# The first loads in two queues, chunk 0 rounded first, and the squares of x behind the third block: a two-block transformer on one core

## The chip, the cores and the metric

The kernel runs on one core of one Trainium2 chip. The metric is the device time in microseconds, the median over timed runs. PE is the matmul engine, DVE the vector engine, ACT the scalar engine, POOL GpSimd; SP is the engine that issues most DMAs.

## What is computed

Two transformer blocks in float32 over 256 tokens of width 1024. Only the very start matters here: the norm of x and the projection with `w_in`.

```python
def rms_norm(x, g):
    xf = x.astype(jnp.float32)
    y = xf * lax.rsqrt(jnp.mean(xf * xf, axis=-1, keepdims=True) + EPS)
    return (y * g.astype(jnp.float32)).astype(x.dtype)

def token_mix(h, w_in, ...):
    p = (h @ w_in).astype(jnp.float32)
    (fox_qkv, fox_f, gdn_qkv, gdn_b, gdn_a, gdn_z, hg_q, hg_f, hg_i, hg_g,
     gla_qk, gla_v, gla_gk, gla_g) = jnp.split(p, _cut_points(IN_SIZES), axis=-1)
...
x = x + token_mix(rms_norm(x, norm1_g[l]), w_in[l], ...) @ w_out[l]
x = x + conv_glu_ffn(rms_norm(x, norm2_g[l]), ...)
```

## The kernel before

Every matmul operand is split in two: a high part, rounded on ACT to the matmul's format (`w_hi`, `h_hi`), and a low part, the remainder, made on DVE (`w_lo`, `h_lo`). A product is then three matmuls: high by high, low weights by high, high weights by low. Weights stream as blocks of 1 MB (128 partitions x 2048 elements, 8 chunks of 256 columns) through a ring of three slots: a DMA into `raw`, ACT's rounding (`split` on ACT, counted by `hi_ready`), DVE's remainder (`split` on DVE, counted by `lo_ready`), and PE's use (counted by `block_used`). SP loads block n when the low part of block n - 3 is done (`weights_in`).

The order of work on every engine is the order in which the code is written; engines meet only at semaphores. x lies in SBUF as 8 chunks of 128 channels by 256 tokens. The norm is not applied to x before the projection: x times the gain of its channel is multiplied, and the result is scaled per token by the reciprocal root `r_1`, which needs the sum of the squares of x over all chunks.

At the start, SP issues the gains (`channel[:, 0:KC]`), then x and the first real block (block 1, slot 1) in four quarters each, alternating, with the small weights (block 0, 28 columns, slot 0) in between, then block 2 in two halves. `first_chunks` on ACT rounds, for each quarter, the weights and two chunks of x, and squares the two chunks. DVE makes the remainders, and sums the squares (`sum_of_three`, `sum_of_last`, `fold_sum`) in between. On PE, `keep_busy` multiplies zeros 13 times, `first_columns` multiplies block 1 chunk by chunk with the small products woven in, `mean_of_x` sums the squares over the partitions by a matmul with ones, and `project(n, f)` multiplies one half (24 matmuls) of block n. ACT's `rstd_x` turns the mean into `r_1` by a logarithm and an exponential. DVE then scales the small products (`small_t`), which PE transposes (`turn_small`, L872) and multiplies (`gk_product`). PE's order from there is project(2, 1), project(3, 0), project(3, 1), gates, and so on; DVE goes on with scaling and convolution taps (L2385) of the projected blocks, which also wait for ACT's first tap and for the masks.

Of the kernel before, what the change touches and what calls it, by code (L numbers as in the profile page):

```python
# [16 lines left out]
P = 128  # L17
# [104 lines left out]
def build(nc, weights, small_in, x_in, masks_in, ident_in, channel_in, row_in, w_gk_in, p_in, table_in,  # L122
# [4 lines left out]
    with ExitStack() as ctx:  # L127
# [318 lines left out]
        def _(sp):  # L446
            sp.dma_start(channel[:, 0:KC], channel_in[:, 0:KC]).then_inc(sem("gains_loaded"), 16)
            for b in range(4):
                sp.dma_start(x[:, 2 * b:2 * b + 2, :], x_in[:, 2 * b:2 * b + 2, :]).then_inc(sem(f"x_loaded{b}"), 16)
                quarter = slice(b * BLK // 4, (b + 1) * BLK // 4)  # L450
                sp.dma_start(raw[:, 1, quarter], weights[0][:, quarter]) \
                    .then_inc(sem(f"x_loaded{b}") if b < 3 else raw_loaded[1], 16)
                if b == 0:
                    sp.dma_start(raw[:, 0, 0:KC * SMALL], small_in).then_inc(raw_loaded[0], 16)
            for half, done in enumerate((sem("half_loaded"), raw_loaded[2])):
                part = slice(half * BLK // 2, (half + 1) * BLK // 2)
                sp.dma_start(raw[:, 2, part], weights[1][:, part]).then_inc(done, 16)
# [78 lines left out]
        def _(pe):  # L536
# [296 lines left out]
            def first_columns():  # L833


                def small_products(k):
# [7 lines left out]
                    if k == KC - 1:  # L844
                        last.then_inc(block_used, 1)

                for k in range(KC):
                    if k % 2 == 0 and k < 6:
                        pe.wait_ge(sem("quarter_lo"), k // 2 + 1)
                    for lo in range(2):  # L850
                        pe.wait_ge(lo_chunk if lo else hi_chunk, k + 1)
                        if k == 6 and lo == 0:
                            block_ready(1)
                        a = h_lo if lo else h_hi
                        for f in range(2):
                            at = slice(k * 256 + f * P, k * 256 + (f + 1) * P)
                            o = PS[:, 5, f * TOK:(f + 1) * TOK]
                            last = add(o, w_hi[:, 1, at], a[:, k, :], k == 0 and f == 0 and lo == 0, k == KC - 1 and lo == 1)
                            if lo == 0:
                                add(o, w_lo[:, 1, at], a[:, k, :])  # L860
                    if k >= 2 and k < KC - 1:
                        small_products(k - 2)
# [2582 lines left out]
```

## Time and profile before

| what | value |
|---|---|
| median of 3 timed runs | 1015.18 us (1014.27 to 1016.13) |
| span of the profiled execution | 1012.9 us |
| median less span (issue and end around the span) | 2.3 us |
| PE busy | 999.3 us, 99% of the span |
| DVE, ACT busy | 846.0 us (84%), 618.7 us (61%) |
| HBM traffic | 174 GB/s over the span |

The profiled execution has no timed figure of its own; its span stands beside the median of the timed ones. In a timeline row the first figure is the start in us, the second the time from the start of the first to the end of the last instruction of the row; "idle before <-releaser" is how long the engine stood before it and what ended that. Neighbouring instructions of an engine overlap a little, so the distance of two starts is the better price of one.

### The profile page before, as it was taken

The page shows a single profiled execution, that of the slowest core. Times are in us where ns is not written, and L with a number is a line of the kernel's source. Part 1 is how long each engine was busy: PE and PEld are TensorE (multiplying, and loading weights), DVE is VectorE, ACT ScalarE, POOL GpSimd, SP SyncE. Part 2 cuts the span into 40 slices and gives each one's busy share as a digit, 9 for nine tenths or more (in the row PEclk, how much of TensorE's full clock was granted, in tenths as well). Part 3 has the DMA queues.
Part 4 walks back from the last instruction along what each step waited for, and adds up shares of the span by engine and source line. Part 5 has one row for each costly group of instructions (what it writes and reads, how often), then busy time and mean ns, then how long its engine had stood idle before and what let it go on. Part 6 is the DMA issues. An engine that isn't in the chain of part 4 may idle for free.

```text
span 1012.9 us, 20813 instructions
## 1 busy us (share of the span) xinstructions
PE 999.3 (99%) x8343; PEld 935.8 (92%) x8343; DVE 846.0 (84%) x1217; ACT 618.7 (61%) x852; POOL 5.8 (1%) x16
## 2 busy tenths in 40 slices
PE   8999999999999999999999999999999999999996
PEld 7998999999999998899999999999999999999985
DVE  6974896899988878869999888799776899988876
ACT  6753565657565655457565556675676666555565
POOL 0000000000000000000000000000000000000000
PEclk9999999999999999999999999999999999999998
DMA  8533315455555545657656555345445356655531
GB/s 328 185 117 96 126 48 176 166 206 172 209 202 171 202 149 184 208 209 231 213 172 209 203 173 201 125 167 184 150 132 174 129 173 210 209 201 186 187 125 42
DMA packets 26498, 175.99 MB, mean 174 GB/s; under 512 B 3229, under 2 KB 3509, under 8 KB 6080
## 3 DMA queue, kind: packets, MB, share of 16 engines
q1 hardware_dynamic: 25616, 171.31, 48.6%
q0 software_dynamic: 816, 3.73, 1.3%
q8 instruction: 50, 0.82, 0.3%
q14 instruction: 16, 0.13, 0.0%
HBM read 173.97 MB, written 2.63 MB: 174 GB/s over the span
## 4 chain that ended last, share of the span: by engine, by line
PE 84%; DVE 7%; ACT 3%; issue 2%; DMA 2%; SPq 0%; DVEq 0%; ACTq 0%
PE PS L587 71%; PE PS L538 12%; DVE w_lo L2244 2%; ACT w_hi L1503 2%; DMA arena<-masks_in 1%; DMA raw<-weights 1%; DVE arena L3051 1%; DVE arena L3024 1%; DVE arena L2385 1%; PE PS L1408 0%; DVE arena L3062 0%; DVE arena L2795 0%; DVE arena L3061 0%; DVE arena L3045 0%; DVE arena L3041 0%
## 5 line engine op out<-in xcount | busy, mean ns | idle before, releaser
L587 PE MATMUL PS<-h_store,w_hi 128*128 128x256 f32 (+1 forms) x1840 | 478.2, 338 | 1.3 <-DVE w_lo L2299 0.9
L2244 DVE TENSOR_TENSOR w_lo<-raw,w_hi 128x2048 fp32r<-128x2048 f32 x154 | 352.5, 2290 | 52.4 <-ACT w_hi L1503 47.2
L587 PE MATMUL PS<-h_store,w_lo 128*128 128x256 f32 (+1 forms) x1400 | 369.5, 281 | 0.2
L1503 ACT ACTIVATE w_hi<-raw 128x2048 fp32r<-128x2048 f32 x156 | 297.9, 1910 | 79.1 <-PE PS L587 64.4
L587 PEld LDWEIGHTS PS<-h_store,w_hi 128*128 128x128 f32 x1840 | 305.3, 187 | 41.0 <-DVE w_lo L2299 1.3
L587 PEld LDWEIGHTS PS<-h_store,w_lo 128*128 128x128 f32 (+1 forms) x1400 | 254.8, 188 | 0.8 <-DVE h_store L2858 0.6
L587 PE MATMUL PS<-act_hi,w_hi 128*128 128x256 f32 x704 | 195.7, 280 | 0.1
L587 PE MATMUL PS<-act_hi,w_lo 128*128 128x256 f32 x704 | 195.1, 279 | 0.1
L587 PE MATMUL PS<-act_lo,w_hi 128*128 128x256 f32 x704 | 192.0, 279 | 0.0
L587 PEld LDWEIGHTS PS<-act_hi,w_hi 128*128 128x128 f32 x704 | 132.3, 188 | 1.6 <-DVE act_hi L2858 0.6
L587 PEld LDWEIGHTS PS<-act_hi,w_lo 128*128 128x128 f32 x704 | 132.3, 188 | 0.3 <-DVE act_hi L2858 0.3
L587 PEld LDWEIGHTS PS<-act_lo,w_hi 128*128 128x128 f32 x704 | 130.5, 188 | 0.0
L1926 ACT ACTIVATE arena<-PS 128x512 f32<-128x512 f32 x51 | 30.2, 592 | 86.8 <-PE PS L587 86.8
L587 PE MATMUL PS<-w_hi,h_store 128*128 128x256 f32 (+1 forms) x352 | 71.4, 307 | 0.4 <-issue 0.4
L1918 ACT ACTIVATE arena<-arena,channel 128x256 f32<-128x256 f32 x132 | 63.6, 531 | 13.3 <-DVE arena L2952 12.0
L2929 DVE SCALAR_TENSOR_TENSOR arena<-arena,channel 128x254 f32<-128x254 f32 x132 | 58.0, 481 | 7.6 <-DVE arena L2925 0.3
L2925 DVE SCALAR_TENSOR_TENSOR arena<-arena,channel 128x255 f32<-128x255 f32 x132 | 57.7, 479 | 0.4 <-ACT arena L1918 0.4
L587 PEld LDWEIGHTS PS<-w_hi,h_store 128*128 128x128 f32 x352 | 54.4, 188 | 3.4 <-issue 0.4
L2950 DVE TENSOR_TENSOR arena<-PS,arena 128x512 f32<-128x512 f32 x51 | 35.0, 686 | 20.5 <-ACT arena L1926 20.5
L587 PE MATMUL PS<-w_lo,h_store 128*128 128x256 f32 (+1 forms) x176 | 45.7, 302 | 0.4 <-DVE w_lo L2244 0.4
L538 PE MATMUL PS<-h_store,w_hi 128*128 128x256 f32 x256 | 45.4, 279 | 0.0
L538 PE MATMUL PS<-arena 64*64 64x64 f32 (+8 forms) x1356 | 41.5, 224 | 0.0
(361 smaller groups left out, 1106.6 us busy)
## 6 DMA issues: line engine op xcount, KB each, us to landing
raw<-weights SPq DMA_DIRECT2D x155, 1024.0 KB, 4.9
raw<-weights SPq DMA_DIRECT2D x12, 256.0 KB, 3.9
arena<-masks_in SPq DMA_DIRECT2D x1, 1600.0 KB, 12.1
bias_by_key<-bias_by_distance POOLq DMA_DIRECT2D x1, 1536.0 KB, 8.0
x<-x_in SPq DMA_DIRECT2D x4, 256.0 KB, 4.4
raw<-weights SPq DMA_DIRECT2D x2, 512.0 KB, 9.0
arena<-bias_by_key POOLq DMA_DIRECT2D x1, 1024.0 KB, 6.7
result<-arena SPq DMA_DIRECT2D x4, 256.0 KB, 2.1
```

The costliest lines, as they stand in the source:

```text
L538: return pe.matmul(o, lhs, rhs, start=start, stop=stop)
L587: return pe.matmul(o, lhs, rhs, start=start, stop=stop, skip_group_check=True)
L1503: act.activation(w_hi[:, slot, :], raw[:, slot, :], ACT.Copy).then_inc(hi_ready, 1)
L1918: ins = act.activation(dst[:, c, :], src[:, c, :], ACT.Identity, scale=w, bias=b)
L1926: act.activation(low, PS[:, bank:bank + 2, TOK:512], ACT.Copy).then_inc(sem("low_copied"), 1)
L2244: tt(w_lo[:, slot, :], raw[:, slot, :], w_hi[:, slot, :].bitcast(F), ALU.subtract).then_inc(lo_ready, 1)
L2385: mark(stt(dst, PS[:, bank_of_block(n), f * TOK:(f + 1) * TOK - d], ch("gdn_conv", (3 - d) * 6 + 2 * s + f), dst, ALU.mult, ALU.add))
L2925: stt(y[:, c, 1:TOK], src[:, c, 0:TOK - 1], channel[:, bass.ds(col(1) + c, 1)], y[:, c, 1:TOK], ALU.mult, ALU.add).then_inc(ready[0], 1)
L2929: ins = stt(y[:, c, 2:TOK], src[:, c, 0:TOK - 2], channel[:, bass.ds(col(0) + c, 1)], y[:, c, 2:TOK], ALU.mult, ALU.add)
L2950: tt(z, PS[:, bank:bank + 2, 0:TOK], low, ALU.add).then_inc(sem("parts_added"), 1)
L3024: tt(z, PS[:, bank:bank + 2, 0:TOK], low, ALU.add).then_inc(sem("parts_added"), 1)
L3051: mark(stt(y_gate[:, c, back:TOK], y_up[:, c, 0:TOK - back], ch("sc_conv", (2 - back) * 8 + 2 * i + c), y_gate[:, c, back:TOK], ALU.mult, ...
```

## The change

x is now loaded from ACT's own queue, in a first quarter, a second quarter and a half, with the gains between the second quarter and the half. SP's queue carries the first block in two quarters and a half, and block 2 whole. ACT rounds chunk 0 of x before the first weights, and alternates on; the squares of x and their sums move behind the rounding and the remainders of block 2, the rounding of block 3 (`block_hi(3)`) moves ahead of `rstd_x`, and DVE's remainder of block 3 ahead of the scaling of the small products. On PE the order inside a chunk changes, the small products come in two groups of four, and `project(2, 0)` stands ahead of `mean_of_x`.

```diff
@@ -444,17 +444,14 @@
 
         @block.sync
         def _(sp):
-            sp.dma_start(channel[:, 0:KC], channel_in[:, 0:KC]).then_inc(sem("gains_loaded"), 16)
-            for b in range(4):
-                sp.dma_start(x[:, 2 * b:2 * b + 2, :], x_in[:, 2 * b:2 * b + 2, :]).then_inc(sem(f"x_loaded{b}"), 16)
-                quarter = slice(b * BLK // 4, (b + 1) * BLK // 4)
-                sp.dma_start(raw[:, 1, quarter], weights[0][:, quarter]) \
-                    .then_inc(sem(f"x_loaded{b}") if b < 3 else raw_loaded[1], 16)
-                if b == 0:
-                    sp.dma_start(raw[:, 0, 0:KC * SMALL], small_in).then_inc(raw_loaded[0], 16)
-            for half, done in enumerate((sem("half_loaded"), raw_loaded[2])):
-                part = slice(half * BLK // 2, (half + 1) * BLK // 2)
-                sp.dma_start(raw[:, 2, part], weights[1][:, part]).then_inc(done, 16)
+            def first_block(a, b, loaded):
+                sp.dma_start(raw[:, 1, a * 256:b * 256], weights[0][:, a * 256:b * 256]).then_inc(loaded, 16)
+
+            first_block(0, 2, sem("w_loaded0"))
+            first_block(2, 4, sem("w_loaded1"))
+            sp.dma_start(raw[:, 0, 0:KC * SMALL], small_in).then_inc(raw_loaded[0], 16)
+            first_block(4, KC, raw_loaded[1])
+            sp.dma_start(raw[:, 2, :], weights[1]).then_inc(raw_loaded[2], 16)
             sp.dma_start(ident[:, :], ident_in).then_inc(sem("ident_and_channel"), 16)
             sp.dma_start(channel[:, KC:N_PC], channel_in[:, KC:N_PC]).then_inc(sem("ident_and_channel"), 16)
             def weights_in(n):
@@ -842,28 +839,32 @@
                     add(o, w_lo[:, 0, at], h_hi[:, k, :])
                     last = add(o, w_hi[:, 0, at], h_lo[:, k, :], False, k == KC - 1)
                     if k == KC - 1:
-                        last.then_inc(block_used, 1)
+                        last.then_inc(block_used, 2)
 
                 for k in range(KC):
-                    if k % 2 == 0 and k < 6:
+                    at = [slice(k * 256 + f * P, k * 256 + (f + 1) * P) for f in range(2)]
+                    o = [PS[:, 5, f * TOK:(f + 1) * TOK] for f in range(2)]
+                    pe.wait_ge(hi_chunk, k + 1)
+                    if k in (0, 2):
+                        pe.wait_ge(sem("quarter_hi"), k // 2 + 1)
+                    if k == 4:
+                        pe.wait_ge(hi_ready, 2)
+                    for f in range(2):
+                        add(o[f], w_hi[:, 1, at[f]], h_hi[:, k, :], k == 0 and f == 0)
+                    if k in (0, 2):
                         pe.wait_ge(sem("quarter_lo"), k // 2 + 1)
-                    for lo in range(2):
-                        pe.wait_ge(lo_chunk if lo else hi_chunk, k + 1)
-                        if k == 6 and lo == 0:
-                            block_ready(1)
-                        a = h_lo if lo else h_hi
-                        for f in range(2):
-                            at = slice(k * 256 + f * P, k * 256 + (f + 1) * P)
-                            o = PS[:, 5, f * TOK:(f + 1) * TOK]
-                            last = add(o, w_hi[:, 1, at], a[:, k, :], k == 0 and f == 0 and lo == 0, k == KC - 1 and lo == 1)
-                            if lo == 0:
-                                add(o, w_lo[:, 1, at], a[:, k, :])
-                    if k >= 2 and k < KC - 1:
-                        small_products(k - 2)
-                small_products(KC - 3)
-                small_products(KC - 2)
-                small_products(KC - 1)
-                last.then_inc(block_used, 1)
+                    if k == 4:
+                        pe.wait_ge(lo_ready, 2)
+                    for f in range(2):
+                        add(o[f], w_lo[:, 1, at[f]], h_hi[:, k, :])
+                    pe.wait_ge(lo_chunk, k + 1)
+                    for f in range(2):
+                        add(o[f], w_hi[:, 1, at[f]], h_lo[:, k, :], False, k == KC - 1)
+                    if k == 3:
+                        for j in range(4):
+                            small_products(j)
+                for j in range(4, KC):
+                    small_products(j)
 
             def turn_small():
                 pe.wait_ge(sem("ident_and_channel"), 48)
@@ -1217,8 +1218,8 @@
             pe.wait_ge(*once("zeros"))
             keep_busy(13, 4)
             first_columns()
+            project(2, 0)
             mean_of_x(0, 6, sum_1, True)
-            project(2, 0)
             turn_small()
             gk_product()
             project(2, 1)
@@ -1555,23 +1556,31 @@
             def first_chunks():
 
 
+                def high(c):
+                    act.activation(h_hi[:, c, :], x[:, c, :], ACT.Identity, scale=ch(PREP[0], c)).then_inc(hi_chunk, 1)
+
+                def weights_hi(a, b, done):
+                    act.activation(w_hi[:, 1, a * 256:b * 256], raw[:, 1, a * 256:b * 256], ACT.Copy).then_inc(done, 1)
+
+                for b in range(2):
+                    act.wait_ge(sem(f"x_loaded{b}"), 16)
+                    high(2 * b)
+                    act.wait_ge(sem(f"w_loaded{b}"), 16)
+                    weights_hi(2 * b, 2 * b + 2, sem("quarter_hi"))
+                    high(2 * b + 1)
+                act.wait_ge(raw_loaded[0], 16)
+                act.activation(w_hi[:, 0, 0:KC * SMALL], raw[:, 0, 0:KC * SMALL], ACT.Copy).then_inc(hi_ready, 1)
+                act.wait_ge(sem("x_loaded2"), 16)
+                high(4)
+                act.wait_ge(raw_loaded[1], 16)
+                weights_hi(4, KC, hi_ready)
+                for c in range(5, KC):
+                    high(c)
+                act.wait_ge(raw_loaded[2], 16)
+                act.activation(w_hi[:, 2, 0:BLK // 2], raw[:, 2, 0:BLK // 2], ACT.Copy).then_inc(sem("quarter_hi"), 1)
+                act.activation(w_hi[:, 2, BLK // 2:BLK], raw[:, 2, BLK // 2:BLK], ACT.Copy).then_inc(hi_ready, 1)
                 for b in range(4):
-                    act.wait_ge(sem(f"x_loaded{b}"), 32 if b < 3 else 16)
-                    if b == 3:
-                        act.wait_ge(raw_loaded[1], 16)
-                    quarter = slice(b * BLK // 4, (b + 1) * BLK // 4)
-                    act.activation(w_hi[:, 1, quarter], raw[:, 1, quarter], ACT.Copy) \
-                        .then_inc(sem("quarter_hi") if b < 3 else hi_ready, 1)
-                    for c in (2 * b, 2 * b + 1):
-                        act.activation(h_hi[:, c, :], x[:, c, :], ACT.Identity, scale=ch(PREP[0], c)).then_inc(hi_chunk, 1)
-                    if b == 1:
-                        act.wait_ge(raw_loaded[0], 16)
-                        act.activation(w_hi[:, 0, 0:KC * SMALL], raw[:, 0, 0:KC * SMALL], ACT.Copy).then_inc(hi_ready, 1)
                     act.activation(sq4[:, b, :], flat(x[:, 2 * b:2 * b + 2, :]), ACT.Square).then_inc(sem("x_squares"), 1)
-                act.wait_ge(sem("half_loaded"), 16)
-                act.activation(w_hi[:, 2, 0:BLK // 2], raw[:, 2, 0:BLK // 2], ACT.Copy).then_inc(sem("quarter_hi"), 1)
-                act.wait_ge(raw_loaded[2], 16)
-                act.activation(w_hi[:, 2, BLK // 2:BLK], raw[:, 2, BLK // 2:BLK], ACT.Copy).then_inc(hi_ready, 1)
 
             def rstd_x(p, bank, dst, squared=None):
 
@@ -1624,14 +1633,19 @@
                     act.activation(flat(act_hi[:, 2 * b:2 * b + 2, :]), PS[:, 4 + b, :], ACT.Copy).then_inc(sem("mixed_hi"), 1)
 
             flat = lambda v: v.rearrange("p u n -> p (u n)")
+            for at, n in ((0, 2), (2, 2)):
+                act.dma_start(x[:, at:at + n, :], x_in[:, at:at + n, :]).then_inc(sem(f"x_loaded{at // 2}"), 16)
+            act.dma_start(channel[:, 0:KC], channel_in[:, 0:KC]).then_inc(sem("gains_loaded"), 16)
+            act.dma_start(x[:, 4:KC, :], x_in[:, 4:KC, :]).then_inc(sem("x_loaded2"), 16)
             act.preload_act_table_set(TABLES)
             act.wait_ge(sem("gains_loaded"), 16)
             act.wait_ge(*once("eps_set"))
-            first_chunks()
-            rstd_x(0, 6, (r_1, r_1_col))
-
             def block_hi(n):
                 split(n, n % RING, n // RING + 1)
+
+            first_chunks()
+            block_hi(3)
+            rstd_x(0, 6, (r_1, r_1_col))
 
             def tokens_from(n):
 
@@ -1824,7 +1838,6 @@
                 act.activation(a_la[CHUNK:P, :, CHUNK:P], a_packed[CHUNK:P, :, :], ACT.Copy) \
                     .then_inc(sem("diagonals_spread"), 1)
 
-            block_hi(3)
             gdn_last_tap(0, 1)
             gates()
             gk_logs()
@@ -2290,29 +2303,31 @@
                     tt(act_lo[:, 2 * b:2 * b + 2, :], pair(4 + b), act_hi[:, 2 * b:2 * b + 2, :].bitcast(F), ALU.subtract) \
                         .then_inc(sem("mixed_split"), 1)
 
-            for b in range(4):
-                quarter = slice(b * BLK // 4, (b + 1) * BLK // 4)
-                if b < 3:
-                    dve.wait_ge(sem("quarter_hi"), b + 1)
-                else:
-                    dve.wait_ge(hi_ready, 2)
-                tt(w_lo[:, 1, quarter], raw[:, 1, quarter], w_hi[:, 1, quarter].bitcast(F), ALU.subtract) \
-                    .then_inc(sem("quarter_lo") if b < 3 else lo_ready, 1)
+            def first_lo(a, b, done):
+                tt(w_lo[:, 1, a * 256:b * 256], raw[:, 1, a * 256:b * 256], w_hi[:, 1, a * 256:b * 256].bitcast(F), ALU.subtract) \
+                    .then_inc(done, 1)
+
+            for b in range(2):
+                dve.wait_ge(sem("quarter_hi"), b + 1)
+                first_lo(2 * b, 2 * b + 2, sem("quarter_lo"))
                 chunk_lo(0, 2 * b)
                 chunk_lo(0, 2 * b + 1)
-                if b == 1:
-                    dve.wait_ge(hi_ready, 1)
-                    tt(w_lo[:, 0, 0:KC * SMALL], raw[:, 0, 0:KC * SMALL], w_hi[:, 0, 0:KC * SMALL].bitcast(F), ALU.subtract) \
-                        .then_inc(lo_ready, 1)
-                if b == 2:
-                    sum_of_three(0, sum_1)
-            sum_of_last(0, sum_1)
-            fold_sum(sum_1)
-            dve.wait_ge(sem("quarter_hi"), 4)
+            dve.wait_ge(hi_ready, 1)
+            tt(w_lo[:, 0, 0:KC * SMALL], raw[:, 0, 0:KC * SMALL], w_hi[:, 0, 0:KC * SMALL].bitcast(F), ALU.subtract) \
+                .then_inc(lo_ready, 1)
+            dve.wait_ge(hi_ready, 2)
+            first_lo(4, KC, lo_ready)
+            for c in range(4, KC):
+                chunk_lo(0, c)
+            dve.wait_ge(sem("quarter_hi"), 3)
             tt(w_lo[:, 2, 0:BLK // 2], raw[:, 2, 0:BLK // 2], w_hi[:, 2, 0:BLK // 2].bitcast(F), ALU.subtract)
             dve.wait_ge(hi_ready, 3)
             tt(w_lo[:, 2, BLK // 2:BLK], raw[:, 2, BLK // 2:BLK], w_hi[:, 2, BLK // 2:BLK].bitcast(F), ALU.subtract) \
                 .then_inc(lo_ready, 1)
+            sum_of_three(0, sum_1)
+            sum_of_last(0, sum_1)
+            fold_sum(sum_1)
+            split(3, 0)
             dve.wait_ge(sem("x_rstd"), 1)
             dve.wait_ge(block_used, 1)
             tt(small_t, PS[0:SMALL, 7, 0:TOK], r_1[0:SMALL, :], ALU.mult).then_inc(sem("proj_bank_read0"), 1)
@@ -2679,7 +2694,6 @@
                     ins.then_inc(lo_ready, 1)
 
             gdn_scale(0, 1)
-            block_lo(3)
             gates_in()
             gdn_taps(0, 1)
             gk_logits()
```

How the instructions stand on the engines: on ACT, before the change, the first 16 instructions behind the table load are these (h_store is the operand made of x, w_hi the rounded weights, xn where the squares of x go):

```order
L1563 ACTIVATE w_hi<-raw 128x512 [waits x_loaded0,constants,gains_loaded]
L1566 ACTIVATE h_store<-x,channel 128x256 x2
L1570 ACTIVATE xn<-x 128x512
...
L1572 ACTIVATE w_hi<-raw 128x1024 [waits half_loaded]
L1574 ACTIVATE w_hi<-raw 128x1024 [waits raw_loaded2]
L1584 ACTIVATE xn<-PS,eps 128x256 [waits x_ms]
L1584 ACTIVATE xn<-PS,eps 128x4
L1591 ACTIVATE xn<-xn 128x256 [waits act_own]
L1591 ACTIVATE xn<-xn 128x4
L1503 ACTIVATE w_hi<-raw 128x2048 [waits block_used,raw_loaded0]
```

After the change, ACT's start and the same place:

```order
L1637 DMA x<-x_in 128x512 x2
L1638 DMA channel<-channel_in 128x8
L1639 DMA x<-x_in 128x1024
L1640 ACT_TABLE_LOAD
L1560 ACTIVATE h_store<-x,channel 128x256 [waits x_loaded0,constants,gains_loaded]
L1563 ACTIVATE w_hi<-raw 128x512 [waits w_loaded0]
...
L1580 ACTIVATE w_hi<-raw 128x1024 [waits raw_loaded2]
L1581 ACTIVATE w_hi<-raw 128x1024
L1583 ACTIVATE xn<-x 128x512 x4
L1504 ACTIVATE w_hi<-raw 128x2048 [waits block_used,raw_loaded0]
L1593 ACTIVATE xn<-PS,eps 128x256 [waits x_ms]
```

The gains' issue moved behind two pieces of x, the squares (xn<-x) behind block 2, and block 3 (128x2048) ahead of the logarithm (xn<-PS).

On PE, from the end of the first block to the transposes of the small products (L872, later L873), before:

```order
L587 MATMUL PS<-arena,ones 128x256 [waits x_sum,constants]
L587 MATMUL PS<-ones,arena 128x2 x2
L587 MATMUL PS<-h_store,w_hi 128x256 [waits hi_ready]
L587 MATMUL PS<-h_store,w_hi 128x256 x15
L587 MATMUL PS<-h_store,w_lo 128x256 [waits lo_ready]
L587 MATMUL PS<-h_store,w_lo 128x256 x7
L872 MATMUL PS<-ident,arena 128x28 [waits proj_bank_read0,ident_and_channel]
```

and after:

```order
L584 MATMUL PS<-h_store,w_hi 128x256 [waits hi_ready]
L584 MATMUL PS<-h_store,w_hi 128x256 x15
L584 MATMUL PS<-h_store,w_lo 128x256 [waits lo_ready]
L584 MATMUL PS<-h_store,w_lo 128x256 x7
L584 MATMUL PS<-arena,ones 128x256 [waits x_sum,constants]
L584 MATMUL PS<-ones,arena 128x2 x2
L873 MATMUL PS<-ident,arena 128x28 [waits proj_bank_read0,ident_and_channel]
```

The 24 matmuls of block 2 moved from between the mean and the transposes to ahead of the mean.

## Rows read from the trace of the kernel before

**Rows 1.** The page, part 1: busy us, share of the span, instructions.

```profile
PE 999.3 (99%) x8343; PEld 935.8 (92%) x8343; DVE 846.0 (84%) x1217; ACT 618.7 (61%) x852; POOL 5.8 (1%) x16
```

**Rows 2.** Windows: length, busy us of PE, PEld, DVE, ACT, POOL, PEclk, DMA.

```profile
40.00:1012.00 972.00, 962.25 (x8076) 901.68 (x8074) 817.67 (x1162) 590.30 (x802) 4.92 (x9) 1.00 0.49 170
```

**Rows 3.** PE's waits, 0 to 45 us: total, times, longest.

```profile
PE PS L587 <- DVE w_lo L2299: 0.9, 2, 0.6
PE PS L587 <- DVE w_lo L2244: 0.4, 1, 0.4
PE PS L587 <- DVE w_lo L2305: 0.2, 1, 0.2
```

**Rows 4.** PE's timeline, 1 to 22 us.

```profile
1.51 5.79 PE L587 MATMUL PS<-zeros_r 128*128 128x512 f32 x13 [1.51 <-POOL zeros_r L512]
...
17.38 0.59 PE L587 MATMUL PS<-arena,ones 128*128 128x256 f32 x2
...
18.18 0.37 PE L587 MATMUL PS<-h_store,w_hi 128*128 128x256 f32 x1
...
21.18 0.31 PE L872 MATMUL PS<-ident,arena 28*128 28x28 f32 x2
```

**Rows 5.** The chain that ended last, 0 to 45 us: start, length, what.

```profile
3.10 4.92 DMA raw<-weights
...
11.47 12.12 DMA arena<-masks_in
...
39.40 1.21 PE PS L587 x8
```

**Rows 6.** DMA issues at 0.76, 5.00, 5.98 and 10.52 us: KB, us to landing.

```profile
channel<-channel_in SPq DMA_DIRECT2D x1, 4.0 KB, 1.8
...
raw<-weights SPq DMA_DIRECT2D x1, 256.0 KB, 7.8
...
raw<-weights SPq DMA_DIRECT2D x1, 512.0 KB, 9.4
...
raw<-weights SPq DMA_DIRECT2D x1, 1024.0 KB, 8.4
```

**Rows 7.** ACT's timeline, 5 to 21 us.

```profile
5.72 0.63 ACT L1563 ACTIVATE w_hi<-raw 128x512 fp32r<-128x512 f32 x1 [3.69 <-DMA raw<-weights]
...
9.38 0.37 ACT L1569 ACTIVATE w_hi<-raw 128x224 fp32r<-128x224 f32 x1
9.66 0.62 ACT L1570 ACTIVATE xn<-x 128x512 f32<-128x512 f32 x1
10.18 0.61 ACT L1563 ACTIVATE w_hi<-raw 128x512 fp32r<-128x512 f32 x1
10.70 0.90 ACT L1566 ACTIVATE h_store<-x,channel 128x256 fp32r<-128x256 f32 x2
11.50 0.61 ACT L1570 ACTIVATE xn<-x 128x512 f32<-128x512 f32 x1
...
14.71 1.05 ACT L1572 ACTIVATE w_hi<-raw 128x1024 fp32r<-128x1024 f32 x1
...
19.43 1.90 ACT L1503 ACTIVATE w_hi<-raw 128x2048 fp32r<-128x2048 f32 x1
```

**Rows 8.** DVE's timeline, 11 to 27 us.

```profile
11.44 0.87 DVE L2257 SCALAR_TENSOR_TENSOR h_store<-x,channel,h_store 128x256 fp32r<-128x256 f32 x2
12.23 0.68 DVE L2264 TENSOR_TENSOR arena<-xn 128x512 f32<-128x512 f32 x1
...
15.80 0.42 DVE L2276 TENSOR_TENSOR arena<-arena 128x256 f32<-128x256 f32 x1
16.14 1.22 DVE L2312 TENSOR_TENSOR w_lo<-raw,w_hi 128x1024 fp32r<-128x1024 f32 x1
...
19.56 0.41 DVE L2318 TENSOR_TENSOR arena<-PS,xn 28x256 f32<-28x256 f32 x1 [1.07 <-ACT xn L1591]
...
21.37 2.29 DVE L2244 TENSOR_TENSOR w_lo<-raw,w_hi 128x2048 fp32r<-128x2048 f32 x1 [0.79 <-ACT w_hi L1503]
...
23.96 2.68 DVE L2385 SCALAR_TENSOR_TENSOR arena<-PS,channel,arena 128x255 f32<-128x255 f32 x6
```

## The prediction

> **What bounds the kernel now.** I read the share of busy time first [rows 1]: PE is busy for 99% of the span and no other engine comes near. From 40 us to the end PE is busy 962.25 of 972 us, at a granted clock of 1.00 [rows 2]. Nothing downstream waits for a fixed time, so whatever PE gains or loses in the first 40 us arrives at the end nearly whole. Next I read whom PE waited for in those 40 us [rows 3]: 0.9 us for the low parts of the first weights and 0.4 us for the low part of one later block; a further 0.2 us went to the small weights. Apart from the start at 1.51 us, that is all that a better start can win. The matmuls on zeros that fill PE run from 1.51 for 5.79 us, to 7.30 [rows 4], so PE cannot start real work much before 7 us even if the data are there.
>
> The chain that ended last passes, before 39.40, through DVE and the masks' DMA, not through PE [rows 5]. PE stood idle for 0.4 us in front of 39.40 [rows 3]. So a PE that reaches that place up to 0.4 us later loses nothing, and beyond that loses one for one.
>
> **The change, part by part.** The span is 1012.9 us and the median of the timed runs 1015.18, so 2.3 us lie around the span; none of the edits touches those. I work out the shift of the span and add it to 1015.18. (A difference under about 0.2%, 2.0 us, can't be told from none here.)
>
> *Loads.* The first x and the first weights are now issued side by side, x from ACT's queue. x went out at 1.21 before, behind the gains at 0.76; now at about 0.75. That is 0.46 us. But the gains of the norm were first in line and landed 1.8 us after issue [rows 6]; now they are third on ACT's queue, behind two pieces of x, and ACT's first instruction still waits for them. Before, the fourth of the 256 KB pieces (issued at 3.10) landed at 8.02 [rows 5]. The gains now have the same four pieces ahead of them or beside them, only not the small weights: 8.02 - 0.46 - some 0.4 for the small weights, about 7.1. From below: if the gains came through with the first piece, ACT starts at about 5.0 (the first pair was ready at 5.72 [rows 7], less 0.46 and a little). From above: 8.0. I take 7.1, because rows 5 has just this amount of data. So ACT's first rounding starts 1.4 us later than the 5.72 of before, and what loads sooner does not help it.
>
> The Trainium skill has two rules on this (page "DMA: Bandwidth & Descriptors"): under "Queues, rings and completion order", each DMA engine consumes its descriptors in ring order; under "Issuing engines are not separate DMA queues", issuing from several engines saves only the sequencer's issue time. The trace before has only one hardware queue in this stretch, so it can't show the second. By the page's rules the gains land behind x and the second queue is worth the issue time alone, which is the case that I forecast; without them the early bound of 5.0 would have weighed more.
>
> *ACT, up to the last weights.* From 7.1: chunks 0 to 4 of x at 0.40 each (a pair starts at 10.70, the next work at 11.50), two pieces of weights at 0.52, the small weights 0.28, the half block 0.95 to 1.05 [rows 7]: 4.3 us, to 11.5. The second half of the weights landed at 12.8 before (5.00 + 7.8 [rows 6]); with fewer and larger pieces and the earlier start I put it at about 11, just in time.
>
> *PE, first block.* The low parts follow on DVE: the half block, 1.22, is done at 12.8. PE has done chunks 0 to 3 and half of the small products by then, and from 12.8 needs 4 chunks and 12 small products: 24 + 12 matmuls. A run of 24 takes 3.0 us (18.18 to 21.18 [rows 4]), so this ends at about 17.0 to 17.3; before it ended at 17.38. Here all of the apparent head start is already gone.
>
> *Block 2 and the mean.* PE goes on with the first half of block 2: 3.0 us, to about 20.0 to 20.3. Its mean of the squares waits for DVE's sums. ACT: block 2 landed at 15.4 (5.98 + 9.4 [rows 6]); I take 14.3 for the earlier start and the larger pieces, with 13.3 and 15.4 as bounds. Two halves at 1.0 make 16.3, four squares at 0.52 make 18.4 [rows 7]. DVE: two low halves from 15.3, 1.2 each, to 17.7; three sums at 0.7 and the fold 0.42: 20.2 [rows 8]. The mean therefore starts at about 20.2 instead of 17.38.
>
> *The new wait.* Before, PE did the mean (17.38), then three microseconds of block 2, and needed the result only at 21.18. The way from the mean through ACT's logarithm and exponential to DVE's scaling of the small products took 17.38 to 19.56, 2.2 us [rows 4, 8], and lay wholly beside block 2. Now block 2 comes first and PE has nothing between the mean and the small transposes. The cover is gone. Moreover block 3 is rounded ahead of both: ACT 18.4 + 1.9 = 20.3 (its data landed at 18.9, 10.52 + 8.4 [rows 6]), DVE 20.3 + 2.29 = 22.6, just later than 20.2 + 2.2 = 22.4. Then the scaling, 0.41: 23.0. PE's transposes start at 23.0 instead of 21.18: **1.8 us later**. On PE this shows as an idle time of some 2 us behind the mean; queued there are the small products' transposes, the gk product and the second half of block 2, and behind them all other blocks.
>
> *DVE's own chain.* From DVE's scaling (19.56) to the convolution taps (23.96) it took 4.4 us, of which 2.29 were block 3 [rows 8], which is now done earlier. 22.6 + 2.1 = 24.7, so the taps start 0.7 to 0.8 later. The masks landed at 23.59 (11.47 + 12.12 [rows 5]) and won't be later than that by much, the same bytes coming through engines that are always fed. So DVE's chain arrives at 39.4 + 0.8, PE at 39.0 + 1.8 = 40.8: PE is the later one.
>
> *Edits at nothing.* ACT's four DMA issues and its table load fit in before the gains land at 7.1 (and would delay ACT only if they took over 4 us); the same number of squares, sums and matmuls is done; the small products moved in pieces of four cost nothing, as PE was waiting anyway.
>
> **Sum:** +1.8 for the transposes, less the 0.4 us that PE idled before 39.40: +1.4, so 1015.18 + 1.4 = **1016.6 us**.
>
> **Rivals.**
> *A gain (faster than before, but under the 0.2%).* The gains don't queue behind x, ACT starts at 5.0 and all loads come 2 us sooner. ACT's work to the last weights is then done at about 9.5, PE runs without a gap from 7.0 and ends the first block at 15.4, and DVE, at 10 us of work behind the half block's rounding (1.2 + 1.7 + 2.4 + 2.5 + 2.3 with small waits), has the scaling done at about 20.5. The transposes start 0.4 to 0.7 us earlier; with the 0.4 of idle time before 39.40 gone as well, if DVE's chain follows, 1014.3. The point that decides is ACT's first rounding at 5.2 or before. For it: the gains are 4 KB. Against it: they are issued third. Chance 0.08, and most of it still inside 0.2%.
> *No change at all.* The loads come about 1 us sooner than I assume and the mean starts at 19.3: transposes at 21.8, 0.2 to 0.6 later, hidden in the 0.4 of idle time: 1015.4. Chance 0.27.
> *Block 3 is late.* Its rounding now stands ahead of the mean's logarithm on ACT and of the scaling on DVE. Its DMA goes out only after the small weights' low part, which comes later than 10.52 now, at 11.5 or so. If it lands after 18.4, each microsecond is one on PE: at 21.5 instead of 18.4 the transposes start at 26.1 (21.5 + 1.9 + 2.3 + 0.4), +4.9 less 0.4: 1019.7. For it: block 3 took 8.4 us before. Against: the queue is full by then anyway. Chance 0.10, with a milder form (landing at 20.0, +3.0: 1018.2) inside it.
> *The clock falls* in PE's gaps: two stretches, 7.3 to 10 and 21 to 23, have PE half idle or idle, and no row before 40 us shows a wait on PE over 0.6 us, with the clock at 1.00. At 1.2 instead of 2.4 GHz the 24 matmuls of a half block would cost up to 3 us more than their 3.0, 1018.5 or above. Chance 0.05.
> My forecast, with its own range of 1015.9 to 1017.8, keeps 0.50.
>
> **Numbers.** Slower by over 0.2% means above 1017.2: all of the last two rivals, 0.15, and a sixth to a fifth of my own case, 0.10: 0.25. Faster by over 0.2% means under 1013.15, which even the best bound does not reach; only a scatter of the timed runs (1014.27 to 1016.13 before) can: 0.04. The rest, 0.71, is no measurable change. The range leaves out the worst of the late cases and the best of the early one: 1014.8 to 1018.4.
>
> **What would show it.** Right: ACT's first rounding starts at about 7 us behind x; PE's first real matmul after 7.5; PE idle for 1.5 to 2.5 us between the mean and the small transposes, and no wait of PE's between the first block and block 2; transposes at about 23; PE's wait before the query block (39.40) gone. Wrong: a first rounding at 5; transposes at or before 21.2; an idle time of PE that is ended by ACT or DVE in front of block 2; a granted clock under 1.00 before 30 us. The prediction fails most easily by the loads' landing times, of which the two queues' share is nowhere shown before.

## The result, and the profile after

The changed kernel takes **1019.49 us** (median of 5 runs, 1017.95 to 1019.56) against 1015.18 before; the ratio is 1.0041, with a 95% interval of 1.0030 to 1.0051. It is slower by 4.3 us, three times the forecast 1.4, and outside the range. The span of the profiled execution grew from 1012.9 to 1017.5 us.

PE's waits in the first 50 us of the changed kernel (total, times, longest) answer to [rows 3]:

```profile
PE PS L584 <- ACT w_hi L1563: 2.0, 1, 2.0
PE PS L873 <- DVE arena L2333: 1.8, 1, 1.8
PE PS L584 <- POOL zeros_r L509: 1.5, 1, 1.5
PE PS L584 <- DVE w_lo L2307: 0.2, 1, 0.2
```

The two forecast gaps are there, one at the start and one between the mean and the transposes (L873), and nothing else; the wait before the query block is gone. But waits of 4.0 us against 1.5 before (start apart) are 2.5 more, and the span grew by 4.6. The windows tell where the rest went (columns as in [rows 2]; the figure before the last two is the granted clock, the number behind PE's busy time its matmuls). In the changed kernel:

```profile
7.10:10.00 2.90, 1.05 (x4) 0.88 (x5) 1.32 (x3) 2.38 (x6) 0.00 (x0) 0.90 1.04 429
10.00:14.00 4.00, 4.00 (x26) 3.94 (x25) 3.16 (x7) 3.44 (x8) 0.00 (x0) 0.65 0.88 288
26.00:30.00 4.00, 4.00 (x24) 4.00 (x23) 3.34 (x11) 2.89 (x9) 0.00 (x0) 0.57 0.75 317
```

The same two stretches of the kernel before:

```profile
10.00:14.00 4.00, 3.78 (x33) 3.49 (x32) 3.60 (x8) 3.26 (x8) 0.00 (x0) 1.00 0.97 362
26.00:30.00 4.00, 4.00 (x37) 4.00 (x36) 3.40 (x17) 2.89 (x7) 0.00 (x0) 1.00 0.72 301
```

From 10 to 14 and from 26 to 30 us PE is busy all the time in the changed kernel and does 26 and 24 matmuls in 4 us, where at full clock it does up to 37. The granted clock was down at 1.2 GHz, half of the full 2.4, for most of both stretches. The share of busy time doesn't show this; the count in a window, the time of a run of matmuls and the clock do. In slices of half a microsecond (changed kernel, the same columns) one sees when the clock fell:

```profile
9.50:10.00 0.50, 0.50 (x2) 0.50 (x3) 0.50 (x2) 0.50 (x2) 0.00 (x0) 0.50 1.13 467
12.50:13.00 0.50, 0.50 (x5) 0.50 (x4) 0.31 (x1) 0.50 (x3) 0.00 (x0) 0.68 1.63 298
26.00:26.50 0.50, 0.50 (x7) 0.50 (x6) 0.18 (x2) 0.50 (x3) 0.00 (x0) 0.98 0.78 328
26.50:27.00 0.50, 0.50 (x4) 0.50 (x4) 0.50 (x2) 0.50 (x1) 0.00 (x0) 0.50 1.13 475
```

It was at 0.50 from about 9.5 to 12.7 and from 26.5 to 29.9 us, so it fell when PE, after its gap, had been at work again for 0.7 and 1.7 us. In PE's timeline, which answers to [rows 4]:

```profile
1.51 5.32 PE L584 MATMUL PS<-zeros_r 128*128 128x512 f32 x13 [1.51 <-POOL zeros_r L509]
8.79 0.47 PE L584 MATMUL PS<-h_store,w_hi 128*128 128x256 f32 x2 [1.95 <-ACT w_hi L1563]
...
22.05 0.59 PE L584 MATMUL PS<-arena,ones 128*128 128x256 f32 x2
...
24.78 0.28 PE L873 MATMUL PS<-ident,arena 28*128 28x28 f32 x2 [1.80 <-DVE arena L2333]
24.91 0.69 PE L535 MATMUL PS<-arena 16*128 16x128 f32 x4
25.52 3.02 PE L584 MATMUL PS<-h_store,w_hi 128*128 128x256 f32 x16
28.34 1.81 PE L584 MATMUL PS<-h_store,w_lo 128*128 128x256 f32 x8
29.99 0.40 PE L584 MATMUL PS<-h_store,w_hi 128*128 128x256 f32 x2
```

The transposes start at 24.78 for 21.18, 3.6 us later, and the 24 matmuls of block 2's second half (25.52 to 29.99) take 4.5 us for the 3.0 of [rows 4]. From there on PE is about 5 us behind.

The loads, and ACT's first work (answering to [rows 6, 7]): first the x pieces issued at 0.75 and the gains, KB and us to landing; then ACT's timeline.

```profile
x<-x_in ACTq DMA_DIRECT2D x1, 256.0 KB, 4.3
...
channel<-channel_in ACTq DMA_DIRECT2D x1, 4.0 KB, 5.9
```

```profile
7.62 0.51 ACT L1560 ACTIVATE h_store<-x,channel 128x256 fp32r<-128x256 f32 x1 [3.59 <-DMA channel<-channel_in]
...
11.21 0.51 ACT L1560 ACTIVATE h_store<-x,channel 128x256 fp32r<-128x256 f32 x1 [0.56 <-DMA x<-x_in]
...
19.51 1.92 ACT L1504 ACTIVATE w_hi<-raw 128x2048 fp32r<-128x2048 f32 x1 [1.66 <-PE PS L584]
23.02 0.63 ACT L1593 ACTIVATE xn<-PS,eps 128x256 f32<-128x256 f32 x2 [1.59 <-PE PS L584]
```

The first x was there at 5.05 (0.75 + 4.3), but ACT waited for the gains until 7.6 (1.69 + 5.91, as the chain has it), 1.9 us later than before. The sum of the squares came when forecast (19.86 + 0.42 = 20.3 below, for 20.2), but PE reached its mean only at 22.05. In DVE's timeline, answering to [rows 8]:

```profile
19.86 0.42 DVE L2289 TENSOR_TENSOR arena<-arena 128x256 f32<-128x256 f32 x1
21.46 2.29 DVE L2257 TENSOR_TENSOR w_lo<-raw,w_hi 128x2048 fp32r<-128x2048 f32 x1 [1.17 <-ACT w_hi L1504]
24.22 0.41 DVE L2333 TENSOR_TENSOR arena<-PS,xn 28x256 f32<-28x256 f32 x1 [0.47 <-ACT xn L1600]
```

### The profile page after: what moved, and what is told of

It is laid out like the page before. It is cut to its first block, busy times and chain, and to the rows that moved or that the text cites. A ratio compares the mean times of both kernels' runs of the same rounds, so it can differ in the third digit from the quotient of the medians.

```text
span 1017.5 us, 20806 instructions
## 1 busy us (share of the span) xinstructions
PE 1001.6 (98%) x8343; PEld 938.4 (92%) x8343; DVE 845.9 (83%) x1216; ACT 619.0 (61%) x851; POOL 5.9 (1%) x16
## 4 chain that ended last, share of the span: by engine, by line
PE 94%; DVE 3%; ACT 2%; DMA 1%; issue 0%; ACTq 0%; DVEq 0%
PE PS L584 81%; PE PS L535 12%; DVE w_lo L2257 1%; ACT w_hi L1504 1%; DMA channel<-channel_in 1%; PE PS L1409 0%; DVE arena L2809 0%; DVE h_store L2872 0%; PE PS L815 0%; PE PS L785 0%; ACT arena L1827 0%; ACT arena L1626 0%; PE PS L947 0%; PE PS L957 0%; ACT L2114 0%
```

## The experiments

The theory, after the result: the change costs by its waits about what was summed, and the rest because PE's clock falls behind both new gaps. Rivals: only the loads, or only the order of the mean, do it; or the slow stretches lie beside waits and cost nothing. "Before" ran beside each group, with medians of 1014.66, 1014.63 and 1014.80, against 1015.18 beside the changed kernel, which was timed only in that first group. So medians of different groups are some 0.5 us apart for no cause in the kernel; below, each run is compared with the "before" beside it, and the ratios carry an uncertainty of about 1 us either way.

| run | us, median (range) | ratio to before, 95% |
|---|---|---|
| changed kernel | 1019.49 (1017.95 to 1019.56) | 1.0041 [1.0030, 1.0051] |
| loads_alone | 1016.33 (1015.61 to 1017.65) | 1.0018 [1.0010, 1.0027] |
| loads_start_fill | 1015.63 (1015.17 to 1016.52) | 1.0009 [1.0000, 1.0018] |
| squares_alone | 1017.41 (1015.43 to 1018.95) | 1.0024 [1.0013, 1.0034] |
| squares_gap_fill | 1015.66 (1014.88 to 1017.12) | 1.0007 [0.9998, 1.0016] |
| both_fill | 1016.29 (1016.07 to 1016.90) | 1.0017 [1.0008, 1.0026] |
| start_fill | 1017.83 (1016.32 to 1018.86) | 1.0033 [1.0021, 1.0044] |
| gap_fill | 1017.72 (1016.33 to 1018.82) | 1.0037 [1.0022, 1.0051] |
| gains_first | 1017.79 (1017.18 to 1018.72) | 1.0031 [1.0019, 1.0042] |
| gains_from_sp | 1017.42 (1015.48 to 1019.36) | 1.0027 [1.0015, 1.0038] |
| mean_first | 1017.43 (1016.67 to 1018.31) | 1.0026 [1.0016, 1.0036] |
| mean_first_fill | 1017.28 (1017.00 to 1018.31) | 1.0024 [1.0015, 1.0033] |
| small_later | 1014.45 (1013.77 to 1015.00) | 0.9995 [0.9986, 1.0004] |

**The two halves of the change apart.** `loads_alone` is the kernel before with the new DMA issues on SP and ACT; on ACT only the waits follow them, and PE and DVE are untouched. From its diff:

```diff
-                    act.wait_ge(sem(f"x_loaded{b}"), 32 if b < 3 else 16)
-                    if b == 3:
-                        act.wait_ge(raw_loaded[1], 16)
+                    if b < 3:
+                        act.wait_ge(sem(f"x_loaded{b}"), 16)
+                        act.wait_ge(sem(f"w_loaded{b}") if b < 2 else raw_loaded[1], 16)
...
```

> The kernel before with the new loads only (x and gains from ACT's queue, gains third; first weights in two quarters and a half; block 2 whole), squares, sums, block 3 and PE's order as before. Waits-and-clock theory: ACT's first rounding at 7.6 as in the changed kernel, PE's first real matmul 1 to 1.5 us later than before behind a 1.3 us gap, the mean at 18.5 to 19.5, no gap behind the mean: 1016.2 to 1017.2 (1 to 2 us slower). Rival, that only the order of the mean costs: no change, 1015.2.

Slower by 1.7 us, within the theory's range. Its first rounding started at 7.94, PE had a gap of 1.9 us in front of its first real matmul, the granted clock was 0.59 from 10 to 14 us, and the mean came at 19.59 for 17.38, with no gap behind it.

`squares_alone` keeps the old loads and moves the squares and their sums, block 3 and the mean (the lines that move the squares on ACT aren't shown here):

```diff
-                        last.then_inc(block_used, 1)
+                        last.then_inc(block_used, 2)
...
-                last.then_inc(block_used, 1)
...
-            mean_of_x(0, 6, sum_1, True)
             project(2, 0)
+            mean_of_x(0, 6, sum_1, True)
...
+            first_chunks()
+            block_hi(3)
+            rstd_x(0, 6, (r_1, r_1_col))
...
+            sum_of_three(0, sum_1)
+            sum_of_last(0, sum_1)
+            fold_sum(sum_1)
+            split(3, 0)
```

> The kernel before with its old loads; only the squares and sums moved behind block 2, block 3 ahead of the mean's logarithm and of the scaling, block 2's first half ahead of the mean on PE. Waits-and-clock theory: PE starts at 7.1 as before and at full clock, the transposes start at about 23.5 behind a gap of 2.5 us, and the clock falls behind that gap: 1018.8. If only waits cost and the clock does not: 1017.2. Rival, that the late first rounding is the whole cause: 1015.2.

1017.41 by the median, 2.4 us slower by the ratio; the profiled run took 1017.93. The forecast of 1018.8 for a fallen clock is too high for the median and fits the upper end of a wide range, 1015.43 to 1018.95; the median is nearer to the 1017.2 that had been expected if only the waits cost. The profile shows the clock's fall, its price only the run with a filler below. PE's waits and windows in it:

```profile
PE PS L871 <- DVE arena L2318: 2.3, 1, 2.3
PE PS L587 <- DVE w_lo L2299: 1.8, 2, 1.3
```

```profile
10.00:14.00 4.00, 3.59 (x29) 3.32 (x30) 2.88 (x8) 2.73 (x7) 0.00 (x0) 1.00 0.95 337
...
26.00:30.00 4.00, 4.00 (x23) 4.00 (x23) 3.55 (x16) 2.82 (x9) 0.00 (x0) 0.57 0.78 324
```

The start is at full clock, also behind its gap of 1.3 us; behind the gap of 2.3 us the clock falls, and 23 matmuls fit in 4 us. So each of the two parts has a gap of its own. Neither is the whole cause, and both rivals of one cause fall. Neither run has the rest of the change: chunk 0 of x rounded first, PE's order inside a chunk, and the small products in two groups. As 1.8 and 2.4 us make up the whole 4.1, these cost nothing that shows here.

**The clock apart from the waits.** These add matmuls on zeros where PE stands idle, and take away no wait. `both_fill`, in the changed kernel:

```diff
-            keep_busy(13, 4)
+            keep_busy(22, 4)
...
             mean_of_x(0, 6, sum_1, True)
+            keep_busy(8, 3)
             turn_small()
```

> The changed kernel with 9 more matmuls on zeros at the start (22 for 13) and 8 of them (512 columns) between the mean and the transposes, to keep the clock up; no wait is taken away. Waits-and-clock theory: granted clock 1.00 through the first 40 us, the 24 matmuls behind the transposes in 3.0 us and not 4.5, the first block done 1 us earlier: 2.7 us saved, 1016.8. Rival, that the waits alone cost and the slow stretches lie beside them: 1019.5.

1016.29: 1.7 us above before by the ratio, where the changed kernel is 4.1 above, so 2.4 less, from 17 matmuls of no use (2.7 less if the medians above their own "before" are compared, 1.6 for 4.3). The saving forecast was 2.7, and the runs lie within 0.8 us of each other. Windows of this run:

```profile
10.00:14.00 4.00, 4.00 (x34) 3.75 (x35) 3.82 (x9) 4.00 (x9) 0.00 (x0) 1.00 0.82 280
26.00:30.00 4.00, 4.00 (x37) 4.00 (x36) 3.52 (x16) 2.83 (x9) 0.00 (x0) 1.00 0.85 356
```

34 and 37 matmuls in the windows that had 26 and 24. ACT's first rounding started at 8.02 here and PE's first real matmul at 9.20, both later than in the changed kernel, and the transposes still stand 2.8 us behind the mean (21.14 to 23.95): no wait was taken away. The rival that the slow stretches cost nothing falls.

`start_fill` and `gap_fill` are one of the two lines each.

> The changed kernel with 22 matmuls on zeros at the start for 13, nothing else. Clock theory: no slow stretch from 9 to 13 us, the first block done about 1 us earlier, the gap behind the mean and the slow stretch behind it stay: 1018.3. Rival, that the start's slow stretch lies beside waits for DVE: 1019.3.

> The changed kernel with 8 matmuls on zeros between the mean and the transposes, nothing else. Clock theory: the transposes start where they do in the changed kernel (24.8), the 24 matmuls behind them take 3.0 and not 4.5 us: 1017.9. Rival, that the clock behind the gap costs nothing in the end: 1019.4.

1017.83 and 1017.72, each 1.1 to 1.2 us closer to its "before" than the changed kernel by the medians, but only 0.8 and 0.4 by the ratios, 1.0033 and 1.0037. Their intervals overlap with the changed kernel's, so neither alone is clear of the noise; only the two together are. In start_fill the clock was 1.00 to 22 us and 0.65 from 26 to 30. In gap_fill the theory met something that it doesn't explain:

```profile
7.10:10.00 2.90, 0.50 (x3) 0.32 (x3) 0.77 (x2) 1.83 (x5) 0.00 (x0) 1.00 1.07 436
10.00:14.00 4.00, 4.00 (x33) 3.78 (x34) 3.36 (x7) 3.64 (x8) 0.00 (x0) 1.00 0.90 287
```

PE's gap at the start was 3.1 us here, the longest of all, and yet the clock held in that execution, the fastest of its five (1016.33 us; the others 1017.39 to 1018.82). So the fall is not sure behind a gap, and the other four executions point the same way: the mean clock over the whole execution was 0.999 in this one and 0.994 to 0.997 in them. In gains_from_sp it was 0.997 in the fastest execution (1015.48) and 0.995 in the two slowest. This accounts for a part of the spread of the kernels with unfilled gaps, 1.5 to 3.9 us; not for all of it, since "before" itself spreads over 2.5 and 2.7 us in 26 and 32 executions, with hardly any relation to its clock.

The same fillers on the two halves:

```diff
-            keep_busy(13, 4)
+            keep_busy(22, 4)
```

> The kernel before with the new loads alone and 22 matmuls on zeros at the start for 13. Clock theory: full clock from 9 to 14 us, the mean at about 18.9 and not 19.6; the late first rounding is left as the only cost: 1015.5. Rival, that the clock has no part in loads_alone: 1016.3.

```diff
             mean_of_x(0, 6, sum_1, True)
+            keep_busy(8, 3)
             turn_small()
```

> The kernel before with the squares part alone (as in the run squares_alone) and 8 matmuls on zeros between the mean and the transposes. Clock theory: full clock after the gap, what is left is the lost cover alone: the transposes at 24.0 as in squares_alone, 2.8 later than before, less what the blocks behind absorb: 1016.5, and the runs lie within 1.2 us of each other. Rival, that the clock's fall is not what spreads and lifts squares_alone: 1017.4.

1015.63 and 1015.66, by the ratios 0.9 and 0.7 us above before. In loads_start_fill the mean was at 19.05. In squares_gap_fill the transposes were at 22.54, not at the 24.0 expected, as the mean came sooner in that run (19.75 for 20.69); so a part of its gain over squares_alone is earlier loads and not the clock. The 1016.5 expected for squares_gap_fill was too high. With the clock held, the loads cost 0.9 us, the order of the mean 0.7, and both 1.7: they add up. The first two are at the edge of the noise (their intervals begin at 1.0000 and 0.9998). Without fillers they cost 1.8, 2.4 and 4.1 (by the ratios, on 1015).

**Can the late start be taken away alone?** `gains_first` puts the gains ahead of x on ACT's queue, `gains_from_sp` ahead of the weights on SP's:

```diff
+            act.dma_start(channel[:, 0:KC], channel_in[:, 0:KC]).then_inc(sem("gains_loaded"), 16)
             for at, n in ((0, 2), (2, 2)):
                 act.dma_start(x[:, at:at + n, :], x_in[:, at:at + n, :]).then_inc(sem(f"x_loaded{at // 2}"), 16)
-            act.dma_start(channel[:, 0:KC], channel_in[:, 0:KC]).then_inc(sem("gains_loaded"), 16)
```

> The changed kernel with the gains issued first on ACT's queue. Waits-and-clock theory: ACT starts at about 5.1, PE's real work at about 6.9 with no gap, full clock up to the mean; the gap behind the mean stays at 1.9 us, since DVE's work still ends at about 23: 1018.0 if the clock falls there, 1016.6 if it does not. Rival, that the late start is the whole cause: 1014.5 to 1015.2. Rival, that it costs nothing: 1019.5.

```diff
+            sp.dma_start(channel[:, 0:KC], channel_in[:, 0:KC]).then_inc(sem("gains_loaded"), 16)
             first_block(0, 2, sem("w_loaded0"))
```

> The changed kernel with the gains issued from SP's queue ahead of the weights, x alone on ACT's queue. If only the gains' place held ACT back, ACT starts at about 5.3 (the first x landed at 5.05 in the changed kernel), PE has no gap at the start and the clock stays: 1017.8, the rest being the gap behind the mean and its clock. If the two queues' first pieces hold one another back, as the run with the gains first on ACT's queue hints, x lands at about 7 again: 1017.8 to 1019, with PE's gap of 2 us still there at 7 to 9 us; the start times tell the two apart.

Here the explanation that the gains' place holds ACT back fell in part. With the gains first, ACT started at 7.24 all the same, not at the 5.1 expected, and PE's gap stayed (2.1 us); it now waited for x. That the time came near the 1018.0 expected is luck. The first piece of x, issued at 1.19, landed 5.9 us later (landings in gains_first of the pieces issued at 0.75 and 1.2: weights, gains, x):

```profile
raw<-weights SPq DMA_DIRECT2D x1, 256.0 KB, 3.4
channel<-channel_in ACTq DMA_DIRECT2D x1, 4.0 KB, 3.6
...
x<-x_in ACTq DMA_DIRECT2D x1, 256.0 KB, 5.9
```

With the gains on SP, x was first and rounded at 4.24, but then the first weights were late:

```profile
4.24 0.51 ACT L1561 ACTIVATE h_store<-x,channel 128x256 fp32r<-128x256 f32 x1 [0.79 <-DMA x<-x_in]
7.10 0.63 ACT L1564 ACTIVATE w_hi<-raw 128x512 fp32r<-128x512 f32 x1 [2.35 <-DMA raw<-weights]
```

In these three runs (the changed kernel, gains_first, gains_from_sp) whichever piece was issued second on a queue landed at 6.9 to 7.4 us, where before the first pair had been there at 5.72 [rows 7]. A first chunk needs gains, x and weights; with two queues side by side, one of the three is always second. gains_from_sp is 2.7 us slower than before by its ratio. Its profiled execution, the slowest of seven, has the start mended for the most part: PE's first real matmul at 7.88 behind a gap of 0.6 us, full clock, and the mean at 20.33. But block 3's data released ACT only at 19.03, its remainder on DVE ran to 23.2, and DVE's scaling of the small products stood behind it: the gap before the transposes grew to 2.5 us, and the clock was at 0.50 from 24 to about 31. Here the prediction's rival of a late block 3 shows in a mild form.

**Does the mean's place on PE matter?** `mean_first` puts it ahead of block 2's first half again, in the changed kernel; `mean_first_fill` has the start's filler as well, and 8 matmuls on zeros ahead of the mean.

```diff
-            project(2, 0)
             mean_of_x(0, 6, sum_1, True)
+            project(2, 0)
```

> The changed kernel with PE's mean ahead of block 2's first half again, ACT's and DVE's order as changed. Lost-cover theory: PE waits 1.2 us for the sum of the squares (20.3) ahead of the mean, none behind it; the transposes start at about 24.1 and not 24.8 and the clock does not fall there: 2 us saved, 1017.4. Rival, that the order on PE does not matter because ACT and DVE are late in either: 1019.0.

```diff
-            keep_busy(13, 4)
+            keep_busy(22, 4)
...
-            project(2, 0)
+            keep_busy(8, 3)
             mean_of_x(0, 6, sum_1, True)
+            project(2, 0)
```

> The changed kernel with 22 matmuls on zeros at the start, PE's mean ahead of block 2's first half, and 8 matmuls on zeros ahead of the mean, where PE waits for the sum of the squares. If the sum (at 20.0 us, DVE's last of five pieces of work) is the bound at full clock, the order on PE is worth nothing: 1016.3, as with both fillers and the changed order. If the lost cover is the bound: 1015.3.

mean_first took 1017.43, as expected, but not for the reason given (its profiled run took 1018.31). PE's wait moved ahead of the mean (1.6 us for DVE's sum), the clock fell behind this gap too, 0.57 from 22 to 26, and the transposes came at 26.29, not at 24.1; block 2's second half then ran at full clock. mean_first_fill, at 1017.28, is 0.7 us above both_fill by the ratios (their intervals overlap), and both values that had been expected are too low. In its profiled run the gains landed at 8.2 and the second half of x at 12.5 (11.2 in the changed kernel), so the sum was there at 21.6 (20.0 in both_fill), the mean started at 21.77, and block 2 had to follow before the transposes, at 25.62. That is 1.7 us later than in both_fill, and the sum was 1.6 later. So the two runs don't tell which place of the mean is the better one once the sum is late: without fillers the old place measured better (1.0026 for 1.0041), with them worse (1.0024 for 1.0017). Why the loads are later in this run is open.

**A small step from the kernel before.** `small_later` issues the small weights behind the second quarter:

```diff
-                if b == 0:
+                if b == 1:
                     sp.dma_start(raw[:, 0, 0:KC * SMALL], small_in).then_inc(raw_loaded[0], 16)
```

> The kernel before with the small weights issued behind the second quarter of x and weights instead of behind the first. The second quarter lands 0.3 us earlier, PE's wait of 0.6 us at 9.4 us shrinks by that: 0.3 us faster than before, 1014.3, less than this measurement tells. Rival, that the small weights then come too late for the small products at 10.6: no change or 0.3 slower.

1014.45 against 1014.80, not to be told from no change. In its profile the waits for the first low parts were 1.4 us and not less than 0.9; the expected mechanism isn't seen. No version beats the kernel before.

## Why the prediction was wrong

*The bound, and that a loss at the start reaches the end: right.* The span grew by 4.6 us: the transposes started 3.6 us later (1.8 had been forecast), 1.5 came behind them, and the 0.4 that PE had idled before 39.40 came off.

*The gains behind x: right in kind, 0.5 us too small.* 7.6 was measured for 7.1, and PE's first real matmul came at 8.79. But the reason was only half right. The early bound of 5.0 rested on the gains alone. gains_first and gains_from_sp show that x or the weights would have come at 7 in their place.

*ACT's and DVE's work: right.* The sum of the squares was ready at 20.3, for 20.2. *PE's own work: too early.* I had PE through block 2's first half at 20.0 to 20.3; it came to the mean at 22.05, so the mean waited for PE and not for the sum.

*The lost cover: right, also in its size.* The wait behind the mean was 1.8 us, for "some 2". ACT's rounding of block 3 waited for PE (1.66 us, until the small products were done), not for its data. With the clock held up in both gaps the kernel is 1.7 us slower than before, and my sum of waits was 1.4. The rival of a late block 3 did not occur in this execution.

*The step that failed* is the last rival: "The clock falls in PE's gaps ... Chance 0.05." I named both places and gave a price, but only as an alternative, and in the sum it stands at nothing, on the ground that the kernel before had no slow stretch. That trace had no wait of PE above 0.6 us after its start, so it could not show what two gaps of 2 us do. The missing term has two parts. Behind the second gap PE's 24 matmuls took 4.5 us for 3.0: 1.5. (Not the "up to 3 us" of the rival, as the clock was down only from 26.5 on.) Behind the first gap, PE took 13.3 us from its first real matmul to the mean, against 11.9, 12.0 and 12.5 in both_fill, gap_fill and start_fill, whose clock held there: 0.8 to 1.3. Together that is 2.3 to 2.8; the fillers take off 2.4 by the ratios. With this term and the 0.5 of the late gains my sum would have been 1.4 + 2.3 to 2.8 + 0.5 = 4.2 to 4.7 us, for 4.3 measured; that the 0.5 reaches the end whole is argued, not shown by a run of its own.

The range failed with it: it held the waits' bounds and the chance for 0.05 of the clock left its price outside.

## What to carry to other kernels

When PE bounds a kernel, price a new gap of PE as the gap plus the slow stretch that may follow it, here 1.5 us behind a gap of 1.8. Look for it by the count of matmuls in a window, since the busy share stays full. If a gap can't be avoided, matmuls on zeros in an unused bank gave back 2.4 us of 4.1 here (by the ratios). It was better still not to open the gap: the kernel before, with its sum of the squares early, the mean ahead of independent work that covers the way back to PE, and x, gains and first weights together at the head of one queue, was faster than every version that has a part of the change.

## What the runs showed that I had not expected

In seven profiled runs the clock fell behind ten gaps of 1.6 to 2.5 us, and in an eighth it held behind one of 3.1; behind gaps of 1.0 and 1.3 (small_later, squares_alone) it held too. Where it fell, it fell at the end of the gap or when PE was at work again, up to some 2 us later. Two queues side by side landed the large pieces as soon on the whole: the first four were there at 7.2 us for 8.0. But the piece second in its queue landed 5.7 to 6.2 us after its issue, where the first three large pieces of the single queue before took 3.6 to 4.1, and the gains, 4 KB, landed at 7.6 from the third place of their queue, where before they were there at 2.6. Loads in two queues cost even with the clock held, by 0.9 us (interval of the ratio 1.0000 to 1.0018). And the granted clock doesn't show every slow stretch: it reads 1.00 from 1.5 us on, yet the 13 matmuls on zeros at the start took 5.3 us in the changed kernel, 0.41 each, where the 8 of the same size in both_fill's gap took 2.1, 0.26 each.
